# Last expert's result added in token rows, and the final norm taken per partition, in a two-layer hybrid decoder with top-2-of-8 experts

## What is computed

```python
logits = (h @ w_router).astype(jnp.float32)
top_vals, top_idx = lax.top_k(logits, TOP_K)            # 2 of 8
gates = jax.nn.softmax(top_vals, axis=-1)
comb = jnp.sum(jax.nn.one_hot(top_idx, N_EXPERTS) * gates[..., None], axis=-2)
for e in range(N_EXPERTS):
    out = out + comb[..., e:e + 1] * swiglu(h, w_gate[e], w_up[e], w_down[e])
...
h = h + moe_swiglu(hn, ...)
return rmsnorm(h, norm_final)      # t * rsqrt(mean(t * t) + EPS) * g
```

## Time and profile before

| | |
|---|---|
| median of 3 runs | 1536.48 us (1534.49 to 1537.03) |
| profiled execution | 1536.4 us, its span 1534.6 us |
| mean granted TensorE clock | 0.981 |
| PE, DVE, ACT busy | 97%, 76%, 60% |
| HBM read | 422.92 MB, 276 GB/s over the span |
| expert stage | about 480 to 1500 us of the span |
| behind the last expert's products | 1500 us to the end |

### The profile page before, as it was taken

How to read it: one execution, slowest core, us unless ns; L and a number is a source line. 1 busy time by engine, 2 the same in 40 slices (tenths; PEclk the granted TensorE clock), 3 DMA queues, 4 the chain that set the end, 5 groups by cost and what they waited for, 6 DMA issues and landing times.

```text
span 1534.6 us, 25503 instructions
## 1 busy us (share of the span) xinstructions
PE 1481.2 (97%) x10730; PEld 1353.3 (88%) x10730; DVE 1169.9 (76%) x1114; ACT 916.8 (60%) x908; POOL 34.1 (2%) x49
## 2 busy tenths in 40 slices
PE   8999999999997999999999999999999999999995
PEld 6799999998887989889888989989988998898983
DVE  6666555557627888888888788888888979888883
ACT  3744334444523766766767676676676766766672
POOL 2020000002000000000000000000000000000000
PEclk9999999999996999999999999999999999999997
DMA  8455555553126999999899999999999989989900
GB/s 317 144 213 206 178 187 193 192 180 123 56 75 246 357 348 344 340 357 346 333 361 374 330 352 356 333 352 353 341 339 361 370 326 346 369 333 347 360 28 29
DMA packets 59425, 425.61 MB, mean 277 GB/s; under 512 B 6961, under 2 KB 7089, under 8 KB 8113
## 3 DMA queue, kind: packets, MB, share of 16 engines
q1 hardware_dynamic: 58464, 422.60, 74.4%
q10 hardware_dynamic: 848, 1.39, 0.3%
HBM read 422.92 MB, written 1.05 MB: 276 GB/s over the span
## 4 chain that ended last, share of the span: by engine, by line
PE 91%; DVE 4%; ACT 2%; issue 1%; POOL 1%; DMA 0%; POOLq 0%; SPq 0%; ACTq 0%; DVEq 0%
PE ps L1700 39%; PE ps L1722 20%; PE ps L1421 10%; PE ps L1443 5%; PE ps L1343 2%; PE ps L1670 2%; PE ps L1688 2%; PE ps L1483 2%; PE ps L1586 1%; PE ps L1707 1%; DVE w_lo L1193 1%; ACT w_hi L641 1%; DVE w_lo L786 1%; PE ps L1375 1%; PE ps L1530 1%
## 5 line engine op out<-in xcount | busy, mean ns | idle before, releaser
L1193 DVE TENSOR_TENSOR w_lo<-ring,w_hi 128x2048 fp32r<-128x2048 f32 x336 | 766.5, 2290 | 131.0 <-ACT w_hi L641 124.9
L641 ACT CAST w_hi<-ring 128x2048 fp32r<-128x2048 f32 x336 | 639.6, 1909 | 270.0 <-PE ps L1700 218.1
L1700 PE MATMUL ps<-w_hi,xg_hi 128*96 128x256 f32 x1792 | 249.3, 281 | 2.5 <-ACT w_hi L641 2.5
L1700 PE MATMUL ps<-w_lo,xg_hi 128*96 128x256 f32 x1792 | 244.4, 278 | 1.0 <-DVE w_lo L1193 0.5
L1700 PE MATMUL ps<-w_hi,xg_lo 128*96 128x256 f32 x1792 | 243.7, 278 | 0.0
L1700 PEld LDWEIGHTS ps<-w_hi,xg_hi 128*96 128x96 f32 x1792 | 223.9, 162 | 16.3 <-DVE xg_lo L1199 2.6
L1700 PEld LDWEIGHTS ps<-w_lo,xg_hi 128*96 128x96 f32 x1792 | 217.3, 162 | 2.6 <-DVE w_lo L1193 2.6
L1700 PEld LDWEIGHTS ps<-w_hi,xg_lo 128*96 128x96 f32 x1792 | 217.8, 162 | 0.0
L786 DVE TENSOR_TENSOR w_lo<-ring,w_hi 128x2048 fp32r<-128x2048 f32 x56 | 129.3, 2311 | 81.8 <-ACT w_hi L461 81.8
L461 ACT CAST w_hi<-ring 128x2048 fp32r<-128x2048 f32 x56 | 106.5, 1903 | 111.7 <-PE ps L1421 92.4
L1722 PE MATMUL ps<-w_hi,ht_hi 128*96 128x512 f32 x448 | 128.0, 407 | 0.0
(11 more groups left out here) (265 smaller groups left out, 1366.9 us busy)
## 6 DMA issues: line engine op xcount, KB each, us to landing
ring<-in_moe_w_gate SPq DMA_DIRECT2D x112, 1024.0 KB, 5.8
ring<-in_moe_w_up SPq DMA_DIRECT2D x112, 1024.0 KB, 5.8
ring<-in_moe_w_down SPq DMA_DIRECT2D x112, 1024.0 KB, 5.9
ring<-in_ffn_w_gate SPq DMA_DIRECT2D x14, 1024.0 KB, 4.9
ring<-in_ffn_w_up SPq DMA_DIRECT2D x14, 1024.0 KB, 4.8
ring<-in_ffn_w_down SPq DMA_DIRECT2D x14, 1024.0 KB, 4.8
ring<-in_lru_w_in SPq DMA_DIRECT2D x7, 1024.0 KB, 12.9
ring<-in_attn_w_qkv SPq DMA_DIRECT2D x6, 1024.0 KB, 4.8
```

The lines of the kernel that those rows point to most:

```text
L641: nc.scalar.copy(w_hi[:, (SPLITS + n) % PARTS], ring[:, s]).then_inc(hi_done, 1)
L1193: V.tensor_tensor(w_lo[:, part], ring[:, ORDER_MOE[n % SLOTS]], w_hi[:, part].bitcast(F32), ALU.subtract).then_inc(lo_done, 1)
L1700: mm = nc.tensor.matmul(ps[0:CAP, c % 2, m * CHF:(m + 1) * CHF], xs[a][:, k], w[b][:, k], start=(k == 0 and (a, b) == (0, 0)), stop=(k == ...
```

## The change

The scatter of zeros for the first expert is dropped, with its `selw`, `weights_back`, zeroed `y_tok` and four adds. Scatters count their experts from `i - 1` now, in the same places of the program.

In `finish` of the last expert TensorE transposes `h` into token rows (`turn_back`: 16 transposes into banks 4, 0, 5, 1) ahead of the last two `down`; ACT and DVE copy two banks each over `h` (`h_rows`). `weights_back` stands between the two `down` and writes bank 6. Right behind the last `down`, `scatter_rows` multiplies `gt` by `y_tok`: four products, 128 tokens by 512 features each. On TensorE the overflow loop stands last. On DVE and ACT it stays ahead of the adds.

With tokens on partitions, the final norm sums squares along the free axis (`accum_out`), takes one root and one reciprocal of 128 x 2, and needs the weight `norm_final` as a row in every partition; this is a new input, read by two DMAs from ACT's queue behind `body(0)`. ACT does a square root of a constant ahead of its loop. The output leaves in four DMAs.

```diff
@@ -206,6 +206,11 @@
...
         out_tok = work[:, :].rearrange("p (b d) -> p b d", b=TT)
+        h_rows = h[:, :, :].rearrange("p c t -> p (c t)").rearrange("p (b d) -> p b d", b=TT)
+        final_row = [xg_mem[:, 0:512], hn_flat[:, 512:1024]]
+        unused = ring[:, SLOTS - 1, :].rearrange("p (n d) -> p n d", n=4)
+        row_sq = small[:, 248:252]
+        row_mean, row_root = small[:, 252:254], small[:, 254:256]
@@ -339,6 +348,10 @@
...
         K_PIECE, V_PIECE, Q_PIECE, O_PIECE = 0, 1, 2, 6
+
+
+        QUARTERS = [(0, 0, 4), (1, 0, 0), (0, 1, 5), (1, 1, 1)]
+        BACK_BANK = 6
         WO_BANK = (1, 2, 3, 4)
@@ -417,11 +430,14 @@
...
-            for b in range(TT):
-                sp.wait_ge(out_even, 2 * (b + 1))
-                sp.wait_ge(out_odd, 2 * (b + 1))
-                sp.dma_start(out[0].rearrange("(b p) d -> b p d", p=P)[b], out_tok[:, b, :]).then_inc(out_sem, 16)
-            sp.wait_ge(out_sem, 16 * TT)
+            for n, (b, m, _) in enumerate(QUARTERS):
+                if n < 3:
+                    sp.wait_ge(out_by_act, n + 1)
+                else:
+                    sp.wait_ge(out_by_dve, 1)
+                sp.dma_start(out[0].rearrange("(b p) d -> b p d", p=P)[b][:, 512 * m:512 * m + 512],
+                             out_tok[:, b, 512 * m:512 * m + 512]).then_inc(out_sem, 16)
+            sp.wait_ge(out_sem, 16 * len(QUARTERS))
@@ -640,9 +656,9 @@
...
-            def weights_back(i):
+            def weights_back(i, bank=4):
                 act.wait_ge(g_turned, i + 1)
-                nc.scalar.copy(gt, ps[0:CAP, 4, 0:T]).then_inc(g_ready, 1)
+                nc.scalar.copy(gt, ps[0:CAP, bank, 0:T]).then_inc(g_ready, 1)
@@ -666,7 +682,6 @@
...
                 split(i, 3)
-                weights_back(i)
                 silu(i, 0, 1)
@@ -691,26 +706,36 @@
...
                 split(i, END_AT + 4)
-                weights_back(i + 1)
+                weights_back(i)
                 silu(i + 1, 0, END_AT + 1 - PIECES)
...
-            def finish(i):
+            def finish(i, first=False):
                 silu(i, NCH - 1, END_AT - 2)
...
                 split(i, END_AT + 1)
+                if first:
+                    for n in range(2):
+                        b, m, bank = QUARTERS[n]
+                        act.wait_ge(h_turned_back, 1)
+                        nc.scalar.copy(h_rows[:, b, 512 * m:512 * m + 512], ps[:, bank, :]).then_inc(h_rows_ready, 1)
+                weights_back(i, BACK_BANK)
                 stage_y(i, END_AT + 1)
...
             body(0, None)
+            act.wait_ge(table_ready, 1)
+            for m in range(2):
+                act.dma_start(final_row[m], norm_final.rearrange("(a d) -> a d", a=1)[:, 512 * m:512 * m + 512].to_broadcast([P, 512])).then_inc(final_in, 16)
             for i in range(E - 1):
...
                 body(i + 1, BODY_AT - 1)
-            finish(E - 1)
+            finish(E - 1, first=True)
+            nc.scalar.activation(row_root, eps_col.to_broadcast([P, TT]), ACT.Sqrt)
             act.wait_ge(table_ready, 1)
@@ -719,12 +744,16 @@
...
                     finish(o + E)
-            weights_back(n_over + E)
-            squares(3, 1)
-            root(1, 0)
-            for g in range(1, 8, 2):
-                act.wait_ge(out_turned, g + 1)
-                nc.scalar.copy(out_tok[:, g // 4, (g % 4) * 256:(g % 4) * 256 + 256], ps[:, g, 0:256]).then_inc(out_odd, 1)
+            for n, (b, m, _) in enumerate(QUARTERS):
+                act.wait_ge(row_added, 4 * n_over + (n + 1))
+                nc.scalar.activation(unused[:, n], h_rows[:, b, 512 * m:512 * m + 512], ACT.Square, accum_out=row_sq[:, n:n + 1]).then_inc(row_squared, 1)
+            act.wait_ge(row_summed, 1)
+            nc.scalar.activation(row_root, row_mean, ACT.Sqrt, bias=eps_col, scale=1.0 / D).then_inc(row_rooted, 1)
+            act.wait_ge(row_rstd, 1)
+            for n, (b, m, _) in enumerate(QUARTERS[:3]):
+                act.wait_ge(row_weighted, n + 1)
+                rows = out_tok[:, b, 512 * m:512 * m + 512]
+                nc.scalar.activation(rows, rows, ACT.Copy, scale=row_mean[:, b:b + 1]).then_inc(out_by_act, 1)
@@ -1146,9 +1175,7 @@
...
                 V.tensor_scalar(sel[:, b], const("iota"), rank[:, b, 1:2], None, ALU.is_equal).then_inc(onehot_ready, 1)
-                V.tensor_scalar(selw[:, b], const("iota"), rank[:, b, 0:1], comb[:, b, 0:1], ALU.is_equal, ALU.mult).then_inc(weighted_ready, 1)
             dve.wait_ge(hn_turned, 4)
-            V.memset(y_tok, 0.0).then_inc(y_staged, 1)
@@ -1227,7 +1254,7 @@
...
-            def body(i, y_at):
+            def body(i, y_at, back=True):
@@ -1238,9 +1265,9 @@
...
                     split(i, n + 2)
-                    if c in (4, 6):
-                        add_back(i, c - 4)
-                        add_back(i, c - 3)
+                    if back and c in (4, 6):
+                        add_back(i - 1, c - 4)
+                        add_back(i - 1, c - 3)
                     if c == 8:
@@ -1257,37 +1284,56 @@
...
-            def finish(i):
+            def finish(i, first=False):
                 gate_times_up(i, NCH - 1)
...
                 split(i, END_AT + 1)
+                if first:
+                    for n in range(2, 4):
+                        b, m, bank = QUARTERS[n]
+                        dve.wait_ge(h_turned_back, 1)
+                        V.tensor_copy(h_rows[:, b, 512 * m:512 * m + 512], ps[:, bank, :]).then_inc(h_rows_ready, 1)
                 stage_y(i, END_AT + 1)
+
+            def add_rows(q):
+                for n, (b, m, bank) in enumerate(QUARTERS):
+                    dve.wait_ge(row_scattered, 4 * q + (n + 1))
+                    rows = h_rows[:, b, 512 * m:512 * m + 512]
+                    V.tensor_tensor(rows, ps[:, bank, :], rows, ALU.add).then_inc(row_added, 1)
...
             lead(0)
-            body(0, None)
+            body(0, None, back=False)
             for i in range(E - 1):
...
                 body(i + 1, BODY_AT - 1)
-            finish(E - 1)
+            finish(E - 1, first=True)
             n_over = dve.value_load(table[0:1, 0:1], min_val=0, max_val=MAX_OVER)
...
                 with dve.If(o < n_over):
+                    add_rows(o)
                     stage_xg(o + E)
                     lead(o + E)
-                    body(o + E, None)
+                    body(o + E, None, back=False)
                     finish(o + E)
-            last = n_over + E
-            for m in range(4):
-                add_back(last, m)
-            dve.wait_ge(added, 4 * last + 4)
-            V.memset(small[:, 160:161], 0.0).then_inc(h_ready, KC)
-            normed(3, "final")
-            for g in range(0, 8, 2):
-                dve.wait_ge(out_turned, g + 1)
-                V.tensor_copy(out_tok[:, g // 4, (g % 4) * 256:(g % 4) * 256 + 256], ps[:, g, 0:256]).then_inc(out_even, 1)
+            add_rows(n_over)
+            dve.wait_ge(final_in, 32)
+            dve.wait_ge(row_added, 4 * n_over + 4)
+            for n, (b, m, _) in enumerate(QUARTERS):
+                cols = slice(512 * m, 512 * m + 512)
+                if n == 3:
+                    dve.wait_ge(row_squared, 4)
+                    link(V.tensor_tensor(row_mean, row_sq[:, 0:2], row_sq[:, 2:4], ALU.add))
+                    V.memset(small[:, 160:161], 0.0).then_inc(row_summed, 1)
+                V.tensor_tensor(out_tok[:, b, cols], h_rows[:, b, cols], final_row[m], ALU.mult).then_inc(row_weighted, 1)
+            dve.wait_ge(row_rooted, 1)
+            V.reciprocal(row_mean, row_root).then_inc(row_rstd, 1)
+            dve.wait_ge(row_rstd, 1)
+            dve.wait_ge(row_weighted, 4)
+            rows = out_tok[:, 1, 512:1024]
+            V.tensor_scalar(rows, rows, row_mean[:, 1:2], None, ALU.mult).then_inc(out_by_dve, 1)
@@ -1653,17 +1699,17 @@
...
-            def weights_back(i):
+            def weights_back(i, bank=4):
...
                 for b in range(TT):
-                    mm = nc.tensor.transpose(ps[0:CAP, 4, b * P:(b + 1) * P], selw[:, b], ident)
+                    mm = nc.tensor.transpose(ps[0:CAP, bank, b * P:(b + 1) * P], selw[:, b], ident)
                 mm.then_inc(g_turned, 1)
...
             def scatter(i, m):
...
                     pe.wait_ge(g_ready, i + 1)
-                    pe.wait_ge(y_staged, 2 * i + 1)
+                    pe.wait_ge(y_staged, 2 * i + 2)
                 if m >= 2:
@@ -1708,11 +1754,11 @@
...
-            def down(i, c, n):
+            def down(i, c, n, first=False):
                 w = [a.rearrange("p (f d) -> p f d", f=2) for a in parts(i, n)]
                 pe.wait_ge(ht_ready, NCH * i + (c + 1))
-                if c == 0:
-                    pe.wait_ge(y_staged, 2 * i + 1)
+                if c == 0 and not first:
+                    pe.wait_ge(y_staged, 2 * i)
                 hs = (ht_hi, ht_lo)
@@ -1727,71 +1773,76 @@
             def lead(i):
...
```

(71 more changed lines are left out.)

## The result

The changed kernel takes 1511.11 us (median of four runs, 1507.78 to 1514.54) against 1535.49 (four runs, 1534.42 to 1537.03). The ratio is 0.9845, 95% interval 0.9820 to 0.9871: 1.6% less time, and more than was forecast. The prediction was 1518.0 with a range of 1513.0 to 1521.5; the measured median lies 1.9 us under the range. The profiled execution took 1514.54 us, its span 1512.7, so it is the slowest of the four.

What follows compares the result with a forecast made beforehand. TensorE was taken to bound the expert stage, with a tail where nothing overlaps. Tail 14.80 less, plus 3.92 for the empty scatter, minus 0.3 for DMAs, gave 18.42 less than 1536.4: 1518.0 us, range 1513.0 to 1521.5.

Steps and rivals of the forecast that it cites:

- stage start: Up to the first gather of the expert stage: one selw leaves the chain, 0.24 us less.
- tail: From the last expert's last product to the span's end: 34.41 us before; new tail ends at 19.61, products ending at 1.9.
- I take 6.94, nearest because it is the same loop.: Behind the last products: VectorE's walk through the overflow loop takes TensorE's old 6.94 us, so adds start at 8.84.
- the short walk: Rival in the tail: VectorE passes its loop early, adds wait for products; 1513.2 us at the floor, 1515.6 halfway; 22%.
- Small terms of the tail: After the walk: adds and weightings 0.69 us each, sum to reciprocal with root and fourth weighting, scalings 0.63 each, then output.
- Table load: ScalarE ahead of the final root: a second load of 1.28 us behind the loop ends near 13.7, hidden before 13.97.
- ScalarE last: Rival in the tail: ScalarE's early table load and root delay its loop and squares; 1518.5 to 1520.8 us; 18%.
- The empty scatter: First expert, body(0): TensorE loses two scatter stretches and one weights_back, 3.68 us; with one selw 3.92.
- The 0.3 for the two DMAs: Two new DMAs on ScalarE's queue hold it up between 0 and 0.9 us; 0.3 taken as cost.
- the clock as a rival: Start of the expert stage: TensorE's clock comes up late and the kernel gets slower than before; 2%.
- The chunks: Gate and up chunks of body(0), 5.62 or 5.46 us: five could change by 0.16 each, 0.8 either way.
- Ahead of the last products: Before the last two down: turn_back's transposes 1.74 us, weights_back 0.22, up to 0.13 won back; products end 1.9 later.

Runs made afterwards that it cites:

- e5: Changed kernel with TensorE going through its overflow loop ahead of scatter_rows instead of behind; 1518.07 us, ratio 0.9885 to the kernel before.
- e7: Changed kernel with two rounds in place of five in the overflow loops of ScalarE and VectorE; 1511.03 us (one run).
- e4: Changed kernel with the whole overflow loop on VectorE and ScalarE behind one question, n_over > 0; 1513.45 us, ratio 0.9851 to the kernel before.
- e3: Changed kernel without the overflow loop and its register on VectorE and ScalarE; 1511.04 us median, ratio 0.9839 to the kernel before.
- e8: Changed kernel with one question ahead of the loop on ScalarE and VectorE and no early constant square root; 1514.21 us, ratio 0.9840.
- e9: Changed kernel with one question ahead of the loop, constant root behind it, sum and root after two weightings in place of three; 1509.03 us, ratio 0.9843.
- e2: Kernel before with only the first expert's empty scatter and its selw, weights_back, zeroed y_tok and adds dropped; 1532.36 us, ratio 0.9971.
- e11: Kernel before, unchanged, timed and profiled a second time; 1535.78 us.
- e1: Changed kernel as it is, timed and profiled again; 1514.26 us median, ratio 0.9859 to the kernel before.
- e10: Changed kernel as it is, timed again and profiled a third time; 1513.53 us, ratio 0.9856 to the kernel before.

## Why the prediction was wrong

In the first profile 21.9 us of span are gone; the sum said 18.42. By the four stretches: stage start +0.74 (forecast -0.24), first expert -5.50 (forecast -3.68), seven experts +2.00 (forecast +2.2: 1.9, and 0.3 for the DMAs, which are issued behind the second gather), tail -19.14 (forecast 34.41 - 17.71 = -16.70).

**The step that failed: "I take 6.94, nearest because it is the same loop."** It is the same loop, but VectorE's first add came 4.82 us behind the last product: 2.1 of the 2.4 us by which the tail was shorter than forecast. Five rounds of 0.70 are 3.5. The rest, 1.3, is VectorE's own copy to `y_tok`, 0.6, which stands ahead of its walk, and 0.7 for reading the register, entering the loop and leaving it. The 6.94 was too long even for TensorE: in e5 it needed 5.3, and what the 1.6 more before consists of is not shown. I had named the short walk as a rival; its middle has the adds end 9.2 us behind the old end of the products, which is what they did (1.9 + 7.31). That the profiled run, 1514.54, came near the rival's 1515.6 is in part luck, as two other stretches missed as well: the first expert gained 1.8 us more than forecast, the stage start 1.0 less.

The rival's reason, the small loop body, is not shown. TensorE's walk over a body some ten times as long took only 0.5 us more (5.3 against 4.82). The Trainium skill ("Runtime: NRT & Kernel Launch", Instruction fetch mechanics) has a taken branch outside the fetched window wait for a fetch. Whether the 0.70 of a round holds such a fetch no run here shows; e7 shows that each round costs it, and e4 that one jump over all of them hides behind the row products. That the floor, the products, was not reached is shown by e3 and e4 (13.22).

**Small terms of the tail.** Adds 2.5 (2.76), three weightings 1.90 (2.07), sum to reciprocal 0.9 (1.19), each shorter, the adds and weightings because such operations back to back overlap by some 0.09 us (four adds take 2.48 us and not 4 x 0.69); scalings 1.95 (1.89). Output 3.1 (2.86): the four DMAs landed after 2.1 us in place of 2.6, yet the end came no sooner, since the last two are issued behind ScalarE's last scaling (it ends at 1509.59, they go at 1509.61 and 1509.98).

**Table load.** Hidden, as forecast, with 0.13 us to spare where the sum had 0.27: the last of three loads ends at 1505.55 + 1.28 = 1506.83, the root starts at 1506.96. The early request bought nothing. The Trainium skill's rule that loads are placed per block ("ScalarE activation tables: per-element evaluation and per-set limits", Table sets in the compiler and the runtime) agrees so far: the load ahead of the loop did not serve the root behind it. But a block need not have a load of its own. In e8 the squares behind the loop run without one. The tail has one load without the early root (e8), without the loop (e3), or with the early root behind the loop (e9).

**ScalarE last.** This rival did not come true. ScalarE left the loop before VectorE, and its load ahead of the squares ended at 1501.43 + 1.28 = 1502.71; the first square, at 1502.97, waited 0.26 us for the first add.

**The empty scatter.** 3.68 was right (e2: 3.5 to 3.7). The 0.3 for the two DMAs was not needed; ScalarE's queue issued them at 598 us, and TensorE has no gap there in the chain. In the profiles of the changed kernel the first expert lasts 105.2 to 106.6, 4.3 to 5.9 less than before. The 0.6 to 2.2 beyond the removed work vary between executions of the same kernel and reach 104.15 (e4) and 108.14 (e8), while e2 and e3 have 107.3 and 107.6. In the first profile they can be counted out: -5.50 is -3.68 for the dropped work, -1.53 for the first 96 products (12.69 in place of 14.22), -0.64 for four chunks at 5.46 in place of 5.62, and +0.35 for the gather (5.77 in place of 5.42). How long these two, the gather and the 96 products, run at a lower clock differs between executions: the gather took 7.13 in e3 and e8 (granted clock 0.50 from 478 to 486 us, 0.79 before), and the 96 products 13.45 in e3 and 14.14 in e2. I counted the clock as a rival that could only lose. Gather and 96 products together took 19.64 before and 19.44 in e11; the changed kernel has 18.46, 18.23 (e1) and 19.45 (e10), so it won 1.0 to 1.4 in two profiles and nothing in the third, and e3 and e8 lost 0.9. What decides it is open. The chunks I had put at 0.8 either way.

**Ahead of the last products.** Transposes 1.75 (1.74), `weights_back` 0.22, no waits left in the two `down` (2.79 each). The copies lay beside.

**Clock.** The row products ran at 1.00 and took 3.67. Behind the walk little of this counted: with 6.41, as in e5, the last add would have ended 7.93 us behind the last product in place of 7.31, by an estimate from these rows (0.83 + 6.41 + 0.69). In e5, where TensorE's walk comes first, it counts in full.

**The spread, not in the forecast.** The profiled run, 1514.54, lies inside my range; the median of the four does not, and that is in part the luck of the draw. Over three sessions the changed kernel has 14 runs: four between 1505.8 and 1509.3, ten between 1511.9 and 1516.1, median 1513.3, just inside the range. Two of the first four came from the low group. One profile caught such an execution (e3, 1504.92). Its dense SwiGLU, which no edit touches, runs faster. Stretches of 130 to 330 us in e3 and e1 (length, then PE busy with its number of instructions):
```profile
130.00:330.00 200.00, 200.00 (x1767) 200.00 (x1766) 117.22 (x113) 86.38 (x88) 0.00 (x0) 1.00 0.56 191
```
```profile
130.00:330.00 200.00, 200.00 (x1701) 200.00 (x1700) 111.28 (x104) 82.08 (x81) 0.00 (x0) 1.00 0.54 185
```
TensorE is never idle in either, the clock is 1.00 in both, and 3.9% more instructions pass in e3. The other twelve profiles have 1700 or 1701 of them. By 472 us this execution is 6 to 8 us ahead of the others. That the whole low group is of this kind is argued from one profile, not shown; e4's, 1508.43, has the ordinary 1701 and owes its time to the shorter tail and the shortest first expert, 104.15. The kernel before has such runs too (1525.39 to 1529.86, three of 11 in the last session). Why the products go faster stays open.

**Where the gain came from**, by tails: early scatter without a walk on any engine 34.41 to 24.37, 10.0 less; the row form another 11.15 less, 1.75 spent ahead; the walk that stays on VectorE 2.1 back. With 3.7 for the empty scatter that is 21 of the 21.9 us in the first profile; the rest lies in the start of the expert stage, which varies. How much of the 10.0 is TensorE's walk is not shown apart; e5, which puts it back beside VectorE's, is 5.1 us slower.

## What to carry to other kernels

A runtime loop that is never entered has a price per round on the engine that must pass it (here 0.70 us on VectorE; all five and the entry took TensorE 5.3), and it belongs behind the engine's last useful work or behind one question (13.22 against 15.3 us of tail). At the end of this kernel little overlaps, so count the crossings between engines: the norm along the free axis needs no TensorE and gave 9 us, more than any single instruction in it. When profiles of one kernel differ by several us, cut them at fixed events and compare the stretches that repeat.

## What was not expected of the hardware

At the same granted clock of 1.00 and with no idle time, 16 products of 128x256 in the dense SwiGLU took 1.81 us in one execution (e3) and 1.88 in the others; in the expert stage 48 of them take 5.46 in some chunks and 5.62 in others, and which chunks these are changes between executions. The profile's releaser of an engine that walks a loop can be wrong: 4.10 us were put down to a product done 2.9 us earlier. A square root asked for ahead of a runtime loop, to have its table ready, gave the tail three table loads of 1.28 us in place of one (e4 against e8).
